# Gate tiles of an input projection as Strassen products, placed among the steps of two attention branches

## The reference

```
h = rmsnorm(x) * norm_g
qa, ka, va, qi, wi, ki, za, qb, kb, vb, zb, ga, gb = split(h @ w_in)
oa = sparse attention: an indexer (qi, ki, wi) scores the keys, the 256 best per query are attended to
ob = sliding-window attention, 192 keys per 64-frame chunk, with sinks
ya = (oa * silu(za)) @ w_br_a ;  yb = (ob * silu(zb)) @ w_br_b
x = x + (sigmoid(ga) * ya + sigmoid(gb) * yb) @ w_out ;  y = rmsnorm(x) * final_g
```

## Time and profile before

| | |
|---|---|
| median of 3 runs | 3376.34 us (3376.05 to 3378.57) |
| profiled execution, its own time | 3377.38 us |
| its span, first to last instruction | 3375.6 us |
| mean granted clock of TensorE | 0.967 |
| TensorE, matmuls busy | 3148.7 us, 93% |
| VectorE, ScalarE, GpSimd busy | 1325.3, 850.0, 881.5 us |
| moved by DMA | 308.47 MB, mean 91 GB/s |

### The profile page before, as it was taken

How to read it: one execution, slowest core, us unless ns; L and a number is a source line. 1 busy time by engine, 2 the same in 40 slices (tenths; PEclk the granted TensorE clock), 3 DMA queues, 4 the chain that set the end, 5 groups by cost and what they waited for, 6 DMA issues and landing times. The chain is left out here.

```text
span 3375.6 us, 47356 instructions
## 1 busy us (share of the span) xinstructions
PE 3148.7 (93%) x17837; PEld 2975.9 (88%) x17837; DVE 1325.3 (39%) x2169; ACT 850.0 (25%) x1753; POOL 881.5 (26%) x652
## 2 busy tenths in 40 slices
PE   5999999999999999999999987975778999999997
PEld 5999999999999999999999986754667999978875
DVE  5003362737282721695000007754994111120411
ACT  4112112131312212211011115533653111031422
POOL 1222211122121222122122214422552222143453
PEclk7999999999999999999999998986998999999999
DMA  4232322222222222222633224234325333263442
GB/s 145 81 98 61 84 62 70 79 64 79 59 69 76 61 79 74 58 63 77 103 98 87 80 64 118 57 88 91 69 55 161 117 111 115 72 227 101 143 159 100
DMA packets 356871, 308.47 MB, mean 91 GB/s; under 512 B 34744, under 2 KB 316440, under 8 KB 353224
## 3 DMA queue, kind: packets, MB, share of 16 engines
q1 hardware_dynamic: 328384, 244.02, 25.9%
q10 hardware_dynamic: 28360, 62.72, 6.6%
HBM read 232.31 MB, written 74.43 MB: 91 GB/s over the span
## 5 line engine op out<-in xcount | busy, mean ns | idle before, releaser
L594 PE MATMUL banks<-h_hi,w_in_tile_hi 128*128 128x384 f32 (+3 forms) x3664 | 823.4, 331 | 10.0 <-POOL w_in_tile_lo L464 7.5
L594 PE MATMUL banks<-h_lo,w_in_tile_hi 128*128 128x384 f32 (+3 forms) x3664 | 821.2, 330 | 0.0
L594 PE MATMUL banks<-h_hi,w_in_tile_lo 128*128 128x384 f32 (+3 forms) x3664 | 821.1, 330 | 0.0
L464 POOL TENSOR_TENSOR w_in_tile_lo<-w_in_tile_raw,w_in_tile_hi 128x512 fp32r<-128x512 f32 x312 | 406.2, 1303 | 1541.5 <-ACT w_in_tile_hi L484 1541.5
L594 PEld LDWEIGHTS banks<-h_hi,w_in_tile_hi 128*128 128x128 f32 (+1 forms) x3664 | 633.4, 188 | 23.0 <-POOL w_in_tile_lo L464 8.1
L594 PEld LDWEIGHTS banks<-h_hi,w_in_tile_lo 128*128 128x128 f32 (+1 forms) x3664 | 631.4, 187 | 1.2
L594 PEld LDWEIGHTS banks<-h_lo,w_in_tile_hi 128*128 128x128 f32 (+1 forms) x3664 | 628.5, 187 | 1.6
L484 ACT CAST w_in_tile_hi<-w_in_tile_raw 128x512 fp32r<-128x512 f32 x312 | 192.9, 620 | 1347.2 <-PE banks L594 1264.1
L761 DVE MAX8 top<-score 128x8 f32<-128x384 f32 (+6 forms) x224 | 247.1, 1103 | 33.0 <-DVE score L764 1.1
L764 DVE MATCH_REPLACE8 score<-top,score 128x384 f32<-128x384 f32 (+6 forms) x224 | 242.9, 1084 | 0.0
L2102 PE MATMUL banks<-w_out_tile_hi,m_hi 128*128 128x512 f32 x576 | 226.5, 393 | 14.9 <-DVE m_lo L2032 13.2
(11 more groups left out here) (243 smaller groups left out, 3570.3 us busy)
## 6 DMA issues: line engine op xcount, KB each, us to landing
w_in_tile_raw<-in_w_in SPq DMA_DIRECT2D x312, 256.0 KB, 2.9
product<-spill ACTq DMA_DIRECT2D x70, 544.0 KB, 3.4
w_out_tile_raw<-in_w_out SPq DMA_DIRECT2D x128, 256.0 KB, 3.1
u_b<-product SPq DMA_DIRECT2D x32, 544.0 KB, 6.2
merged<-u_b ACTq DMA_DIRECT2D x16, 544.0 KB, 7.4
x_rows<-in_x_prompt SPq DMA_DIRECT2D x8, 1024.0 KB, 5.3
b_q_raw<-product SPq DMA_DIRECT2D x16, 512.0 KB, 7.5
w_br_tile_raw<-in_w_br_b SPq DMA_DIRECT2D x64, 128.0 KB, 2.9
```

The source lines that it names most:

```text
L464: pool.tensor_tensor(s.w_lo[:, q, :, :], s.w_raw[:, q, :, :], s.w_hi[:, q, :, :].bitcast(F32), ALU.subtract).then_inc(lo_made, 1)
L594: last = pe.matmul(ps[0:m, 3 * slot + c, 0:w], w_[:, q, kq, 0:m], h_[:, k, t0:t0 + w], start=(k == 0 and w_ is s.w_hi and h_ is s.h_hi), s ...
```

## The change

The 32 gate tiles leave the projection. With columns in pairs of tiles (left, right), K in halves of 8 tiles, and tokens in halves (the sample's 64 tokens go with both middle blocks: `place_of` puts them behind token 512), each pair is a 2 x 2 block product, made from seven products (numbered 1 to 7 as Strassen's) instead of eight: 3, 4, 5 and 2 on 576 tokens in two chunks of 288, 1, 6 and 7 on 512. Products 3 and 4 use h as it lies in SBUF and differences of weights; 5 and 2 use single weights and sums of h; 1, 6 and 7 use both mixed. The mixed h (`mixed_hi`, `mixed_lo` in memory) is made in the first gate stage and loaded over the old h later. Results are collected by loads, adds and stores of gate tiles in memory.

Three new stages take the place of the tiles, of the prompt's branch A and of branch B:

- `gates_first`: 32 products (3 and 4), the mixing of h (40 pieces in 23 steps), the turning of key and value blocks, the bias lines.
- `gates_second`: 32 products (5 and 2), in pieces of 12 matmuls, 3 or 4 of them in each step beside one unit of branch B. Branch B has 2 probability buffers instead of 3 and one pair of score banks instead of two; its u goes to memory.
- `gates_third`: 48 products (1, 6, 7), 0 to 2 pieces of 12 matmuls a step beside one unit of the prompt's branch A. Values are multiplied for 2 heads at a time instead of 4, all scaling is on GpSimd.

In the projection z's silu is one activation now, and indexer dots stand in one or two tiles per block, some starting half a tile later; the evacuation stores a tile in three transfers. In `merge` all u comes from memory, and the sigmoid of the gates is on ScalarE.

The diff, cut to what sets the order and the waits of the gate work:

```diff
+OPERANDS = {3: ((0, 1), (1, 1)), 4: ((1, 0), (0, 0)), 5: ((1, 1),), 2: ((0, 0),),
+            1: ((0, 0), (1, 1)), 6: ((0, 0), (0, 1)), 7: ((1, 0), (1, 1))}
...
+STAGES = (side_by_side(3, 4), side_by_side(5, 2), side_by_side(1, 6) + [(7, n) for n in range(GATE_PAIRS)])
...
+    def due(self, at, ahead):
+        return [j for j in range(ahead, len(JOBS))
+                if max(self.ends[j - ahead], self.late if j >= FIRST_JOB[2] else 0) == at]
...
+    def load_weights(self, sp, j):
+        m, n = JOBS[j]
+        if j >= 2:
+            sp.wait_ge(self.lo_made, 2 * (j - 1))
+        for (half, side), ring in zip(OPERANDS[m], (self.s.w_raw, self.s.w_y)):
+            col = GA + (2 * n + side) * P
+            src = self.w_in[0, half * HALF_K * P:(half + 1) * HALF_K * P, col:col + P]
+            sp.dma_start(ring[:, 2 * (j % 2):2 * (j % 2) + 2, :, :].rearrange("p q k c -> p (q k) c"),
+                         src.rearrange("(k p) c -> p k c", p=P)).then_inc(self.raw_in[j % 2], 16)
...
+    def combine(self, eng, j, h):
+        x, y = self.x_half(j, h), self.y_half(j, h)
+        eng.wait_ge(self.raw_in[j % 2], self.raw_count(j))
+        eng.tensor_tensor(x, x, y, ALU.subtract if JOBS[j][0] in (3, 4) else ALU.add).then_inc(self.summed, 1)
+    def split_hi(self, act, j, h):
+        if self.is_sum(j):
+            act.wait_ge(self.summed, 2 * self.sums_before(j) + h + 1)
...
+        if j >= 2:
+            act.wait_ge(self.w_used, 2 * (j - 2) + h + 1)
+        act.copy(self.s.w_hi[:, (2 * j + h) % 4, :, :], self.x_half(j, h)).then_inc(self.hi_made, 1)
+    def split_lo(self, pool, j, h):
+        unit = (2 * j + h) % 4
+        pool.wait_ge(self.hi_made, 2 * j + h + 1)
+        pool.tensor_tensor(self.s.w_lo[:, unit, :, :], self.x_half(j, h), self.s.w_hi[:, unit, :, :].bitcast(F32),
+                           ALU.subtract).then_inc(self.lo_made, 1)
...
+    def sync_step(self, sp, at):
+        for j in self.due(at, 4):
+            self.load_weights(sp, j)
+        for j in range(FIRST_JOB[1], len(JOBS)):
+            if max(self.ends[j - 1], len(STAGES[0])) == at:
+                self.load_parts(sp, j)
+    def scalar_step(self, act, at):
+        self.store_ended(act, at - 1)
+        for j in self.due(at, 2):
+            for h in range(2):
+                self.split_hi(act, j, h)
+    def pool_step(self, pool, at):
+        for j in self.due(at, 3):
+            if j < FIRST_JOB[1]:
+                for h in range(2):
+                    self.combine(pool, j, h)
+        for j in self.due(at, 2):
+            for h in range(2):
+                self.split_lo(pool, j, h)
+    def vector_step(self, dve, at):
+        for j in self.due(at, 3):
+            if j >= FIRST_JOB[2]:
+                for h in range(2):
+                    self.combine(dve, j, h)
+        for j in self.ending(at):
+            if j >= FIRST_JOB[1]:
+                self.add_parts(dve, j)
```

More of the change, by code:

```diff
@@ L321, in project, with steps_at @@
     blocks = list(first_step)
-    def steps_at(b, tile, tiles, k):
-        steps, at, places = score_steps(b), tile * KT + k, tiles * KT
-        return [(first_step[b] + j, *steps[j]) for j in range(len(steps) * at // places,
-                                                              len(steps) * (at + 1) // places)]
+    def steps_at(b, first, places, tile, k):
+        steps, at = score_steps(b), tile * KT + k - first
+        if not 0 <= at < places:
+            return []
+        return [(first_step[b] + j, *steps[j]) for j in range(len(steps) * at // places, len(steps) * (at + 1) // places)]
     with Phase(nc) as ctx:
@@ L470, in _, with relu @@
         def _(act):
-            def relu(b, tile, tiles, q):
+            def relu(b, first, places, tile, q):
                 for k in range(q * KQ, (q + 1) * KQ):
-                    for n, _, _, w in steps_at(b, tile, tiles, k):
+                    for n, _, _, w in steps_at(b, first, places, tile, k):
                         act.wait_ge(dots_done, n + 1)
@@ L572, in dots @@
             def dots(step, h, c, w):
+                for b in blocks:
+                    if step == first_step[b]:
+                        pe.wait_ge(kidx_ready, 4 if b == NB else 3)
+                        pe.wait_ge(q_ready, blocks.index(b) + 1)
                 if step >= 2:
@@ L613, in tile @@
                     def tile(n, j, i):
-                        if kind == "silu" and j % 2:
-                            turn_block(i + (first_turned[col] + 1), P)
                         product(n, (n0 + j) % 2, wait_acc=not isinstance(n, int) or n >= 2,
-                                scored=None if scored is None else (scored, j, count), chunks=chunks_of(col))
+                                scored=None if scored is None else (*scored, j), chunks=chunks_of(col))
                     loop(pe, n0, count, tile)
-                elif what == "bias line":
-                    pe.wait_ge(consts_in, 32)
-                    pe.matmul(ps[0:H_A + H_B, 7, 0:RELS], table, hot, start=True, stop=True).then_inc(line_done, 1)
-                elif what == "turn the sample":
-                    turn_block(0, DEC)
                 elif what == "natural":
@@ L644, in _ @@
                     last.then_inc(kidx_turned, 1)
-                elif what == "scores":
-                    pe.wait_ge(kidx_ready, 4 if x == NB else 1)
-                    pe.wait_ge(q_ready, blocks.index(x) + 1)
         @block.vector
@@ new lines, in spread_pieces @@
+def spread_pieces(stage, lead, costs, tail, piece_us, most):
+    pieces = pieces_of(stage)
+    counts = [4 if stage == 1 else 2] * lead
+    left = len(pieces) - sum(counts) - tail
+    target = (sum(costs) + left * piece_us) / len(costs)
+    given, spent = 0, 0.0
+    for n, cost in enumerate(costs):
+        spent += cost
+        want = round((target * (n + 1) - spent) / piece_us)
+        count = max(0, min(most, want - given, left - given))
+        counts.append(count)
+        given += count
+    rest = len(pieces) - sum(counts)
+    while rest > 0:
+        counts.append(min(most, rest))
+        rest -= counts[-1]
+    out, at = [], 0
+    for count in counts:
+        out.append(pieces[at:at + count])
+        at += count
+    return out
```

1804 lines of the change are left out of this document (1255 added, 549 removed).

## The result

The changed kernel takes 3801.5 us (median of 4 runs, 3799.3 to 3810.0); the kernel before 3377.1 beside it. The ratio is 1.1261, 95% interval 1.1242 to 1.1281: slower by 424 us. The forecast was 3528, its range ended at 3650. The direction was right, the size was not: 273 us are missing from the sum, and no case that the forecast gave a chance reached 3801. The profiled execution (3801.4 us, span 3799.7) shows where.

A forecast was written before the change was run, and what follows sets the result against it. TensorE was taken to bound the kernel, busy nearly all the span. Against 3377.4 us, removals of 768, 9, 219.7 and 232 and additions of 12, 440, 435, 468 and 25 were summed to +151: 3528 us, range 3345 to 3650.

The forecast's parts named there:

- What bounds the kernel before: Whole old kernel: TensorE busy nearly all the span, 1942 of 1951 us in the projection; 117 us of pauses in attention.
- tiles removed: Projection: 32 gate tiles at 24.0 us each go away, -768 us.
- merge: Merge: u of branch B now comes from memory, so the first matmul and pairs of tiles wait, +25 us (10 to 40).
- Step 1: Projection: gate tiles -768 us, moved turns of blocks -9, one new wait +12; the longest selection hidden, at nothing.
- Step 3: First gate stage: weight load and GpSimd's work run serially, period 11.3 us, with mixing and transfers 440 us in all.
- The 4.5 MB of bias lines: +10: First gate stage: storing the bias lines adds 10 us.
- The rule of 512 B: First gate stage's weight load: at line rate 1 MB would move in 2.8 us, stage 35 us shorter; not adopted.
- Step 4: Second gate stage: products between branch B's 34 units, 10.3 us a step, 435 us in all (363 to 500).
- Step 5: Third gate stage: products between 64 units of the prompt's branch A, 6.25 us a step, 468 us (436 to 530).
- The clock: First gate stage: pauses might hold TensorE at 1.2 GHz, some +20 us, chance 0.2; forecast kept the upper level.
- TensorE-bound after all: Rival, gate stages: loads land in time, stages run at TensorE's pace, 232, 363 and 442 us; 3222 us, chance 0.11.
- The queues saturate: Rival, gate stages: loads take 7.5 us or more, stages 500, 500 and 530 us; 3715 us, chance 0.07.

The follow-up runs named there:

- the last kernel: Six of the edits at once, plus gate pieces before a block's first scores, the operand behind the sample's tables, mixed rows over 26 steps: 3471.5 us.
- the kernel with weights first: Changed kernel with GpSimd's low part before the sum and ScalarE's split of the next weights ahead of rounding mixed h, in the first gate stage: 3653.2 us.

## Why the prediction was wrong, point by point

- **What bounds the kernel before; tiles removed; merge; output**: right. Sample, merge and output are within 1 us of the sum; the merge's +25 measured some 24, and a few us more in the sample and one less in the output cancel, which is luck.
- **Step 1, "Their longest piece ... so I cost it at nothing"**: failed, 48 us (33.8 + 11.3 + 3.2 of waits before score products). I looked at the longest selection and asked what hides it. The stall is at the other end, the start of a group: with fewer tiles between them four groups begin 8 K tiles into a pair, while their queries are issued behind that pair's last weights. The kernel with later scores got 29 us of it back. The one new wait that I did price, 12 us, measured 10.2.
- **Step 3, the first gate stage**: the mechanism and its sizes held (plain period 10.9 for 11.3, with mixed rows 13.9 for 13.6 and 12.0, load 5.7 to 5.9 for 5.9), and both orders that I blamed gave the time back when turned round. The term that failed is "The 4.5 MB of bias lines: +10". The measured hole is 66 us less some 10 of ordinary waiting, about 56 us, of which cutting the store up gave 32 back. The forecast gives no working for its 10, and the row of before shows 101 GB/s and a 24.84 us issue behind the store. It was in the trace, hidden under 24 us tiles but for 7.5 us, and I moved it to a place with nothing to hide it. That is about 46 us too little there, and 3 too much in the rest of the stage.
- **The rule of 512 B**: the Trainium skill (DMA: Bandwidth & Descriptors, Specifications) gives 512 B as the smallest transfer that reaches line rate. By my estimate this rule would have made the load 4.7 us; the load that stood bare took 5.7 to 5.9. On this pattern the row was the better guide. But once the waits were gone the same 512 B rows, with mixed rows of 2 KB between them, moved at 313 GB/s, more than the 262 that my row gave: one small transfer shows its landing, not what the queues can carry.
- **Step 4, the second gate stage**: failed, the largest miss, 112 us. I wrote that "z can be issued only behind a weight load that waits for this step's last product" and put it among "transfers" inside 10.3 us. I had both links and never closed the circle: z frees VectorE, this frees GpSimd, this frees the weight load, and that frees z. The times of VectorE, GpSimd and SyncE and the landing of z add up to 13.6 us, while VectorE is busy 37% and GpSimd 35% of the stage. Then 12.0 us a step for 10.3 is 54 us; the other 58 are in the sample's units and the tail, where TensorE stood 25 us at once. With z off the loop 22 of these 58 came back too; the rest is open, since moving the operand gave nothing. The forecast had named 5 us for the 4.2 MB operand and then left them out of its sum: its own terms make 440, and the whole 3533.
- **Step 5, the third gate stage**: failed, 60 us. The steps took 455 us (first values to the end) for 400 + 16; of these 39 us 25 are the seven waits for the split queries at the change of block, which had no term, and 14 stay open. The entry took 73 for 52, and another order of its loads gave nothing, so it may well be bound by bytes. That transfers are "level with" TensorE in the early steps fits: from 2423 to 2599 us the DMA share was 0.91 and TensorE busy 92%.
- **The clock**: the forecast kept the upper level and gave the lower one 20 us. The first gate stage ran at a mean of 0.75; when the waits went, the clock came back to 0.94 by itself in the stretch looked at. TensorE's busy time in this stage was 275 us, and 235 in the last kernel, at 0.89. Since TensorE was not what most of the steps waited for, I take it that little of this was on the path; no run separates it. The Trainium skill (TensorE: Matmul & The Clock Gate, Why this matters for your kernels) warns of such pauses between bursts of matmuls, and the trace agrees on the clock.
- **The rivals**: "TensorE-bound after all" fell, and even the last kernel, with its three stages at 1260 us, is far from the 1037 of that rival. "The queues saturate" fell as a picture of the first two stages (share 0.62 and 0.56), though its time was the nearest, 3715: its 500, 500 and 530 come within 30 us of the measured 483.5, 547.5 and 528.5, for reasons that were mostly not its own. It is the mended kernel in which the queues do saturate, in the first stage. The break-even period of 7.9 us, given under the first rival, doesn't come out of the terms shown: with all other terms kept, 151 us over 29 periods make it 6.1.
- **The range**: it ended 151 us below the time, and had room only for what was listed. Of the four misses three were waits without a term and one, the bias lines, a term of 10 us that measured about 56; all have one sign. A change that takes apart three stages should leave room upwards for what was not seen.

## What to carry to other kernels

Where several engines hand work round, follow each released instruction until you come back to where you started; the sum round the circle is the least that a period through it can take (13.6 us here), and the busy share of no engine shows it. A load that only waits for its buffer belongs ahead of one that waits for another engine, as in the one edit of SyncE's order that gave 98 us. Before a step is moved, look up in the old trace how long its issues took and what hid them: a store that cost 7.5 us under 24 us tiles cost about 56 in a stage with periods of 11. And saved columns are worth nothing here until the bytes that they cost fit under them.

## What was not expected of the hardware

- While two broadcast stores from 8 and 16 partitions (1.5 and 3 MB) were under way, the queues moved 101 to 104 GB/s in all at a share of 0.86 to 0.89, and the next store on the same queue held ScalarE for 24.8 us (before) and 30.0 us (after). In 16 parts, no issue on that queue from 1340 to 1620 us took more than 1.3 us.
- The queues carried 313 GB/s at a share of 0.99 over 155 us with weight rows of 512 B and mixed rows of 2 KB among them (the kernel with weights first).
- Edits in different places gave together the sum of their gains to within 3 us in 310, although one of them brought its stage to the limit of its transfers.
